# A two-layer mixture with 16,384 experts: 96 tokens look their experts' rows up, the other 160 pass all experts in plain float32

## The reference, cut to what matters

```python
def block(xc):                                   # 128 tokens
    q = (xc @ w_q).reshape(PEER_CHUNK, PEER_HEADS, 2, half)
    sc = jnp.einsum('thpd,hpnd->thpn', q, subkeys).astype(jnp.float32)
    s1, i1 = lax.top_k(sc[:, :, 0], PEER_TOPK)
    s2, i2 = lax.top_k(sc[:, :, 1], PEER_TOPK)
    ...
    top, pos = lax.top_k(cand, PEER_TOPK)
    idx = jnp.take_along_axis(cidx, pos, axis=-1).reshape(PEER_CHUNK, PEER_HEADS * PEER_TOPK)
    gate = jax.nn.softmax(top, axis=-1).reshape(PEER_CHUNK, PEER_HEADS * PEER_TOPK)
    u_e = jnp.take(u, idx, axis=0)
    v_e = jnp.take(v, idx, axis=0)
    act = jax.nn.gelu(jnp.einsum('ted,td->te', u_e, xc).astype(jnp.float32))
    return jnp.einsum('te,ted->td', (gate * act).astype(v_e.dtype), v_e)
```

## Time and profile before

| | us |
|---|---|
| median of 3 runs | 2288.14 (2285.95 to 2288.94) |
| span of the profiled execution | 2284.1 |
| PE busy / DVE busy / ACT busy / POOL busy in it | 2268.4 / 1699.0 / 1324.8 / 430.5 |
| u phase, first layer | 257.34 to 654.45 |
| v phase, first layer | 654.45 to 1003.53 |
| u and v phase, second layer | 1175.48 to 1922.82 |
| DMA: bytes moved, mean rate | 408.53 MB, 179 GB/s |

### The profile page before, as it was taken

How to read it: one execution, slowest core, us unless ns; L and a number is a source line. 1 busy time by engine, 2 the same in 40 slices (tenths; PEclk the granted TensorE clock), 3 DMA queues, 4 the chain that set the end, 5 groups by cost and what they waited for, 6 DMA issues and landing times.

```text
span 2284.1 us, 33324 instructions
## 1 busy us (share of the span) xinstructions
PE 2268.4 (99%) x12380; PEld 1929.4 (84%) x12380; DVE 1699.0 (74%) x3098; ACT 1324.8 (58%) x2181; POOL 430.5 (19%) x355
## 2 busy tenths in 40 slices
PE   9999999999999999999999999999999999999999
PEld 9788888888888888887788888888888888877887
DVE  7567588999975555668758898997555666877885
ACT  3454555578765554646555558776555564666554
POOL 1000233178710000000013316872000000000000
PEclk9999999999999999999999999999999999999999
DMA  7455455544455655644455554445556575333555
GB/s 257 156 176 190 161 191 189 183 167 156 149 194 193 203 193 194 231 163 142 141 171 187 193 177 169 153 155 190 194 193 232 184 227 179 135 123 118 185 186 173
DMA packets 112096, 408.53 MB, mean 179 GB/s; under 512 B 12592, under 2 KB 12640, under 8 KB 111680
## 3 DMA queue, kind: packets, MB, share of 16 engines
q1 hardware_dynamic: 107712, 391.63, 50.4%
q0 software_dynamic: 3504, 13.47, 1.7%
q10 hardware_dynamic: 720, 1.31, 0.2%
HBM read 405.30 MB, written 1.05 MB: 178 GB/s over the span
## 4 chain that ended last, share of the span: by engine, by line
PE 87%; DVE 9%; ACT 2%; issue 1%; DMA 1%; POOL 0%; ACTq 0%; DVEq 0%
PE ps L716 24%; PE ps L633 21%; PE ps L705 12%; PE ps L636 11%; PE ps L672 3%; PE ps L669 3%; PE ps L676 3%; DVE lo L1967 3%; PE ps L915 2%; PE ps L768 1%; DVE big L1973 1%; ACT hi L1373 1%; DVE big L2303 1%; PE ps L889 1%; PE ps L616 1%
## 5 line engine op out<-in xcount | busy, mean ns | idle before, releaser
L1967 DVE TENSOR_TENSOR lo<-raw,hi 128x1024 fp32r<-128x1024 f32 (+1 forms) x627 | 765.4, 1224 | 366.1 <-ACT hi L1373 363.6
L1373 ACT ACTIVATE hi<-raw 128x1024 fp32r<-128x1024 f32 x677 | 714.3, 1057 | 479.7 <-PE ps L716 270.7
L633 PE MATMUL ps<-xs,hi 128*128 128x512 f32 x2560 | 650.8, 396 | 1.0 <-DVE big L2918 1.0
L633 PEld LDWEIGHTS ps<-xs,hi 128*128 128x128 f32 x2560 | 459.2, 189 | 83.6 <-DVE big L2918 1.1
L636 PEld LDWEIGHTS ps<-xs,lo 128*128 128x128 f32 x2560 | 349.0, 190 | 25.8
L636 PE MATMUL ps<-xs,lo 128*128 128x256 f32 x2560 | 356.3, 282 | 0.0
L2998 POOL TENSOR_SCALAR lnp<-iota,selT 128x128 f32<-128x128 f32 x256 | 278.1, 1097 | 167.0 <-DVE negT L2345 88.9
L705 PE MATMUL ps<-hi,lefts 128*128 128x512 f32 x986 | 304.0, 389 | 0.0
L716 PE MATMUL ps<-lo,lefts 128*128 128x512 f32 x986 | 303.7, 389 | 0.0
L716 PE MATMUL ps<-hi,lefts 128*128 128x512 f32 x986 | 303.6, 389 | 0.0
L716 PEld LDWEIGHTS ps<-hi,lefts 128*128 128x128 f32 x986 | 184.9, 188 | 38.7 <-DVE lefts L2033 0.2
(11 more groups left out here) (370 smaller groups left out, 2505.8 us busy)
## 6 DMA issues: line engine op xcount, KB each, us to landing
raw<-in_peer_u SPq DMA_DIRECT2D x256, 512.0 KB, 3.2
raw<-in_peer_v SPq DMA_DIRECT2D x256, 512.0 KB, 4.2
raw<-in_ret_vg SPq DMA_DIRECT2D x32, 512.0 KB, 3.2
raw<-in_peer_q SPq DMA_DIRECT2D x24, 512.0 KB, 3.2
raw<-in_ffn_up SPq DMA_DIRECT2D x22, 512.0 KB, 3.3
raw<-in_ffn_down SPq DMA_DIRECT2D x22, 512.0 KB, 4.0
raw<-in_ffn_gate SPq DMA_DIRECT2D x18, 512.0 KB, 4.3
raw<-in_ret_qk SPq DMA_DIRECT2D x16, 512.0 KB, 4.6
```

What stands on the lines that cost most here:

```text
L633: e.matmul(out, uh[:, k, :], xs[:, k, :, :].rearrange("p h t -> p (h t)"), start=k == 0, stop=False)
L1373: e.activation(parts(i)[0][:, 0:w], raw[:, i % N_RAW, 0:w], ACT.Copy).then_inc(s_hi, 1)
L1967: e.tensor_tensor(ul[:, 0:w], raw[:, i % N_RAW, 0:w], uh[:, 0:w].bitcast(F32), ALU.subtract).then_inc(s_lo, 1)
```

## The change

**Two kinds of tokens.** Tokens 0 to 95 (`LOOKED`) look their experts up. Tokens 96 to 255 (`DENSE` = 160) go through all experts as before.

**The dense tokens.** The units of `u` and `v` are no longer split. SP loads them straight into six `plain` places, which lie where `hi` and `lo` were. TensorE multiplies them in plain float32, the expert weights stationary in both phases: in the u phase 8 matmuls of 160 columns for a unit, in the v phase 8 (one for each 128 output features), also of 160 columns. The v phase thus makes its output with features on the partitions. Of the last six units (`LATE`) the second half of the features comes at the end, and the result is turned back on TensorE (`turned_back`, `turn_back`), with the looked-up sums added through a matmul with the identity. Since a turn brings 512 features of both token tiles, neither tile is complete before the last one. The one-hot groups of gates are 40 instead of 64. No halves are copied, added or split in these phases.

**The looked-up tokens.** DVE computes a list of 128 expert numbers for each token (`idx`). POOL issues 256 indirect DMAs in a layer, 128 on `u` and 128 on `v` (`look_up`): each brings one row of 4 KB for each of the 96 tokens, into one of five places (`N_ROWS`). DVE uses each in one instruction over 96 x 1024 (`look`): product and sum with `x` for `u`, multiply and add into `sums` for `v`.

**The order.** `topk` now runs 11 steps at a time until c = 16, the gates are waited for at c = 18, the groups begin at c = 20. Looks: one beside each unit from c = 20 on (88 in the u phase), then two and one in turns beside the v units (168, done by k = 111 of 128). TensorE waits for all 256 looks at k = 122.

The diff, cut:

```diff
+LOOKED = 96
+DENSE = S - LOOKED
+GROUPS = DENSE // 4
+N_PLAIN, N_ROWS, LATE = 6, 5, 6
+LISTED, SPREAD, LOOKS = 18, 20, 20
...
+            n = 0 if c < SPREAD else 1 if j == 0 or c % 8 == 7 else 0
+            steps[c, j] = list(range(at, min(at + n, GROUPS + 2)))
+            at = min(at + n, GROUPS + 2)
+            gathers += [q + N_ROWS] * len(steps[c, j])
+            n = 1 if c >= LOOKS else 0
+            looks[c, j] = list(range(q, q + n))
+            q += n
...
+    for k in range(128):
+        n = min(256 - q, 2 - k % 2)
...
-                    for j in range(2):
-                        feat_wide(n + j, u.view[:, j, :], X_PEER[l])
+                    for j in range(2):
+                        m = 256 * l + 2 * c + j
+                        w = plain[:, m % N_PLAIN, :].rearrange("p (k n) -> p k n", k=8)
+                        e.wait_ge(*plain_landed(m))
+                        for k in range(8):
+                            ins = e.matmul(u.view[:, j * DENSE:(j + 1) * DENSE], w[:, k, :], Peer.xT[:, k, :],
+                                           start=k == 0, stop=k == 7)
+                        ins.then_inc(s_pused, 1)
...
-                acc(f"peer_v{l}", 128, after=after, tail=6, between=between)
+                def blocks(k, first):
+                    w = plain[:, (256 * l + 128 + k) % N_PLAIN, :]
+                    for b in range(4 * first, 8 if first or k < 128 - LATE else 4):
+                        ins = e.matmul(us[b // 2].view[:, b % 2 * DENSE:(b % 2 + 1) * DENSE],
+                                       w[:, b * 128:(b + 1) * 128], experts[:, k, :], start=k == 0 and b % 2 == 0, stop=k == 127 and b % 2 == 1)
+                for k in range(128):
+                    if k == 128 - LATE:
+                        e.wait_ge(*looked(l, 256))
+                        for f in range(2):
+                            e.matmul(ys[f].view, ident[:, :], Peer.sums[:, f * 512:(f + 1) * 512], start=True, stop=False)
+                    e.wait_ge(*plain_landed(256 * l + 128 + k))
+                    ins = blocks(k, 0)
...
+                for k in range(128 - LATE, 128):
+                    blocks(k, 1).then_inc(s_pused, 1)
+                    if k == 124:
+                        turn_back(0)
+                turn_back(1)
...
+                    e.wait_ge(*rows_landed(l, q))
+                    if q < 128:
+                        e.tensor_tensor_reduce(rows, rows, x[0:LOOKED, 0, :], 1.0, 0.0, ALU.mult, ALU.add,
+                                               Peer.act[0:LOOKED, q:q + 1]).then_inc(s_looked, 1)
+                    else:
+                        e.wait_ge(*looked(l, q))
+                        e.scalar_tensor_tensor(out=sums, in0=rows, scalar=weight[:, q - 128:q - 127], in1=sums, op0=ALU.mult,
+                                               op1=ALU.add).then_inc(s_looked, 1)
...
+            def look_up(l, q):
+                table = A[f"peer_ur{l}"] if q < 128 else A[f"peer_v{l}"].rearrange("n p d -> (n p) d")
+                m = 256 * l + q
+                if q >= N_ROWS:
+                    e.wait_ge(*looked(l, q - N_ROWS + 1))
+                e.indirect_dma_start(out=Peer.rows[m % N_ROWS][0:LOOKED, :], out_offset=None, in_=table,
+                                     in_offset=bass.IndirectOffsetOnAxis(ap=Peer.idx[0:LOOKED, q % 128:q % 128 + 1], axis=0)
+                                     ).then_inc(s_row[m % N_ROWS], 16)
...
+            def plain_load(l, i):
+                m = 256 * l + i
+                if i < N_PLAIN:
+                    e.wait_ge(s_used, split_before[m] + 1)
+                else:
+                    e.wait_ge(*plain_used(l, i - N_PLAIN + 1))
+                src = A[f"peer_u{l}"][i] if i < 128 else A[f"peer_v{l}"][i - 128]
+                e.dma_start(plain[:, m % N_PLAIN, :], src).then_inc(s_plain[m % N_PLAIN], 16)
```

401 lines of the change are left out of this document (260 added, 141 removed).

## The result

The changed kernel takes 2573.86 us (2564.42 to 2588.39, 4 runs) against 2287.28 (2285.95 to 2288.94, 4 runs): a ratio of 1.126 (1.122 to 1.130), 12.6% slower. Forecast was 2146, with a range up to 2330.

A forecast was written before the change was run, and what follows sets the result against it. PE bounds both phases before; afterwards PE bounds u (323 us) and transfers bound v (345). Two layers: 2 x 668 + 11 + 4 = 1351 against 1493, 142 less, span 2142, median 2146 us; 8-in-10 range 2085 to 2330.

The forecast's parts named there:

- the rate of the transfers: V phase: 133 MB of units and look-ups move at 404 GB/s, taking 330 us, so the phase goes from PE to transfers.
- signs that I had named of being wrong: Look-ups over 1.5 us on POOL, under 380 GB/s with full engines, landings over 7 us, 160-column units well over 2.24 us.
- The u phase: First phase of a layer: PE sets its time, 311 us plus 3, 4 and 5 of waits, 323 us against 397 before.
- Rival B: Transfers slower than 404 GB/s: 2230 us at 358 GB/s, or 2254 if 96 rows load the paths unevenly; chance 0.25.
- Rival A: Slower look-ups bound POOL: gain gone at 2.1 us each, 2450 us at 2.4; chance 0.26 shared with the change otherwise failing.
- My sum: POOL in the u phase: look-ups 2.4 and one-hot rows 2.0 us, 4.4 of a two-unit step's 5.0 us.
- A plain unit: PE, both phases: 8 float32 matmuls of 160 columns at 0.28 us, 2.24 us a unit.
- The wait for the gates: U phase, c = 18: PE asks after 88.6 us, DVE's topk takes 93, so PE waits about 4 us (0 to 15).
- The hand-off: End of the first v phase: turning back, norm, transposes and halves lie bare, some 11 us.
- The long wait at k = 122: V phase: TensorE waits there for the last look, then still has six units and two matmuls, 15 us.
- rival C: V phase stays with PE if transfers reach 464 GB/s: 289 us, a time of 2034 us; chance 0.09 including anything faster.
- My 330 us for 133 MB: V phase: bytes of 128 units and 168 look-ups at 404 GB/s, ending with the last look.

## Why the prediction was wrong

**The step that failed is the rate of the transfers.** I took 404 GB/s, between 416 and 389, from a stretch in which units of 128 partitions ran with full engines, and carried it over to a mixture with 96-partition transfers. The mixture ran at 279, and a look-up landed a median of 12.5 us after its issue; both were among the signs that I had named of being wrong (under 380 GB/s, over 7 us). With that number the same step gives 133 MB / 279 = 477 us, and the v phase until k = 122 took 1121.66 - 632.36 = 489. The u phase, which I had left with TensorE because 370 GB/s were asked for, was asked for more than 280, and became a phase of transfers as well: 375 us instead of 323. The excess of the first layer is 52 + 168 = 220 us, the whole error 428 for two layers. That the shape of the look-ups is behind the rate is shown by the kernels with 128 rows and with left-out rows; how exactly a 96-row transfer is shared out is inferred.

**Rival B looked in the right place and had a quarter of the price.** It named the 96 partitions and uneven paths, but put the fuller half at its full 202 GB/s: 2254 us, 108 of the 428. The even halves of 48 and 48 rows, at 243 GB/s, showed that it isn't the sum over the paths. With the last 32 rows left out, B's arithmetic did hold for the rate: it gives 133 MB in 384 us, 347 GB/s, and 358 in the program of transfers and 366 in the kernel were measured. The time was 2325 and not 2254 even so; there too the transfers came one for one (122 units and 122 looks from 592.51 to 909.3), and the look-ups left over were done while TensorE stood. The rule of the Trainium skill (SBUF — State Buffer, Door 1: The DMA port swizzle) that I cited behind B isn't contradicted: the 208 GB/s of partitions 0-63 alone are half of 410, as half of the ports would give. No run here shows the ports singly, and the rest of the price, which that rule doesn't give, is in how 96 partitions are shared out. B's chance of 0.25 should have been larger and its upper end open: I had a sign that no row covered this shape, wrote "no run so far bears on it", and closed the range at 2330 all the same.

**Rival A was right in a corner.** A look-up takes POOL 0.93 us (the median; 1.12 in the u phase in the mean), below the 1.2 I took and far below the 2.1 at which it decides alone. But once the transfers were mended, POOL was the slower one in the u phase. A step of two units has two look-ups and 2.25 one-hot rows, since there are nine groups in eight steps, and not one in each as I had counted: 2.25 x 1.15 + 2 x 1.19 and 0.5 us of gaps, 5.5 us by this sum and 5.4 by the 21 groups in 100 us, against 4.9 of TensorE's own. My sum had 4.4 of 5.0; the quarter of a row and the gaps between its instructions were missing, and the spare tenth that I counted on didn't exist. The other rule of the Trainium skill that I cited (SBUF — State Buffer, Who interferes with whom) would lengthen a look-up by up to a look; in the trace half of them took 0.93 us or less and the longest 2.37, so if it struck, it struck some and not most.

**What was right.** A plain unit: 2.17 us (122 in 265.2, in the run without rows) for 2.24; the five units behind the wait for the gates took 11.88 us, 2.38 each, at a granted clock of 0.91. The wait for the gates: 6.5 us for 4. The u phase without rows: 317 us for 323. Looks of 1.24 and 1.28 us for 1.23 to 1.34. The hand-off: from the last unit at 1144.95 to the next layer's first product at 1155.84, 10.9 us for 11. The long wait at k = 122 and full DMA engines from c = 20 on. The floor of 2012 us means that with TensorE alone the change is worth 276 us; rival C had put this at 2034.

**What I would have missed even with the right rate.** With 405 GB/s the kernel took 2249 and not 2146: the streams share one for one, so a phase with more look-ups than units ends in a stretch in which only one of them works: 79 us of waiting in the first layer and 89 in the second. Of these, 66 us come already at k = 90, where the norm of the memory stands behind the looks, a place that the prediction didn't look at. My 330 us for 133 MB supposed that the bytes can be had in any order.

## What to carry to other kernels

A full DMA share doesn't tell the rate: read GB/s beside it, for the very shape of transfer that is to be added, and where no row has that shape, time it before anything is built on it. Let a transfer cover all 128 partitions evenly, if need be with left-out rows; 96 useful rows so fetched are faster than a transfer of 96. When two streams share the engines, count their transfers in each phase, and not the bytes alone: what one has over the other is done at the end, with everyone else waiting. And when an engine falls behind, look for whatever else stands behind the late work in its program: another engine may wait for that, at a place that the change didn't touch.

## What the runs showed of the hardware

- With the DMA engines full (share 1.03) HBM to SBUF ran at 410 GB/s for transfers that stretched evenly over 128 partitions (all, alone and beside units; every other one and every fourth, beside units), and for partial blocks of neighbouring partitions at 208 (0-63), 277 (0-95), 249 (32-127), 275 (0-111). Beside full units these had 262, 287, 279 and 305, and 0-31 had 310, 0-47 and 64-111 in turns 243.
- A left-out row isn't free, but nearly: the pair of a unit and 96 spread rows ran at 406 GB/s instead of 410. Left-out rows still appear as packets, as this line of the kernel with the last 32 left out shows against 20784 such small packets in the kernel after:

```profile
DMA packets 185822, 609.97 MB, mean 263 GB/s; under 512 B 37168, under 2 KB 37216, under 8 KB 185408
```

- POOL's time for an indirect transfer hardly depends on its rows: in the stream program 0.88 us for 64 (42.34 / 48), 0.91 for 96 and 0.92 for 128. With the bound its median was 0.99 in the v phase.
- TensorE's granted clock falls while it waits and comes back late. Around the 78.6 us wait of the kernel with every fourth row left out:

```profile
900.00:925.00 25.00, 0.00 (x0) 0.00 (x0) 19.77 (x17) 0.00 (x0) 19.02 (x15) 0.50 0.78 255
950.00:975.00 25.00, 19.09 (x106) 16.78 (x107) 8.89 (x9) 4.39 (x6) 0.00 (x0) 0.80 0.33 111
```

  The clock is 0.50, 1.2 GHz, while TensorE idles, and 0.80 (2.4 GHz is 1.00) in the mean of the 25 us in which it starts again. The four matmuls behind the wait took 3.78 us, twice the 1.88 of the version without rows, which didn't wait.
